# A decoder layer on one core: half of the attention moved among the expert gathers, and the first part of the mixer rewritten around a transposed x

## The reference, cut to what matters

```python
h = pad(concat([meta_tokens(16), x(1024)]))          # D_MODEL 1024
xn = rms_norm(h, norm1_g)
q, k, v, ga, gg = split(xn @ w_in)                    # 4 heads x (2 x 64), v: 4 x 128, conv: 2 x 512
p = softmax(q @ k.T / 8 - slope[head] * distance)     # causal, two components for each head
a = p[component 0] - lam * p[component 1]
attn = rms_norm(a @ v, attn_subln_g) * (1 - lam_init)
conv = silu(group_norm(depthwise_conv31(ga * sigmoid(gg))))
h = h + concat([attn, conv]) @ w_out
xn2 = rms_norm(h, norm2_g)
# experts, for every token and each of 8 heads:
s = (xn2 @ wq) @ subkeys.T                            # 2 x 128 scores
e = indices of the best 16 of the 16 x 16 best sums
w = softmax(best) * gelu(u_tab[e] . xn2)
h = h + sum(w * v_tab[e])
out = rms_norm(h, final_norm_g)[16:]
```

## Time and profile before

| what | value |
|---|---|
| time, three runs | 3162.5 us median, 3161.84 to 3164.97 |
| profiled execution, its own time | 3164.81 us |
| its span, first to last instruction | 3163.0 us |
| TensorE matmuls busy | 2352.9 us, 74% |
| VectorE busy | 2047.2 us, 65% |
| ScalarE busy | 1364.5 us, 43% |
| POOL busy | 1134.8 us, 36% |
| DMA | 1121.65 MB, mean 355 GB/s |
| mean granted TensorE clock | 0.833 of 2.4 GHz |

### The profile page before, as it was taken

The page is one execution under the profiler, slowest core; times in us unless marked ns, Lnnn a source line. Parts: engine busy times, 40 slices in busy tenths (PEclk is TensorE's granted clock), DMA queues, the critical chain, the costliest instruction groups (busy, mean ns, idle before and its releaser), DMA issues.

```text
span 3163.0 us, 36373 instructions
## 1 busy us (share of the span) xinstructions
PE 2352.9 (74%) x11880; PEld 897.3 (28%) x11880; DVE 2047.2 (65%) x4903; ACT 1364.5 (43%) x4011; POOL 1134.8 (36%) x1073
## 2 busy tenths in 40 slices
PE   8998987677677776777777767776777777777766
PEld 4655554322222222222222222222222222222211
DVE  1566673566666666666666666666666666666664
ACT  3143444344444444444444444444444444444443
POOL 1000000344444444443444434443444444444442
PEclk9999987788888878888888778877888888877776
DMA  3300000999999999999999999999999999999997
GB/s 110 120 27 27 20 7 25 390 426 427 427 426 423 426 426 413 427 425 426 419 418 424 426 424 421 424 427 425 410 425 426 426 414 423 426 424 426 420 426 332
DMA packets 184964, 1121.65 MB, mean 355 GB/s; under 512 B 19520, under 2 KB 45248, under 8 KB 53584
## 3 DMA queue, kind: packets, MB, share of 16 engines
q0 software_dynamic: 147456, 1073.81, 80.9%
q1 hardware_dynamic: 37328, 45.63, 4.3%
HBM read 1110.97 MB, written 8.39 MB: 354 GB/s over the span
## 4 chain that ended last, share of the span: by engine, by line
DMA 55%; PE 14%; ACT 5%; DVE 4%; issue 3%; POOL 2%; SPq 0%; DVEq 0%; ACTq 0%; POOLq 0%
DMA ring<-table,e_odd 28%; DMA ring<-table,e_even 26%; PE acc_odd L1350 5%; PE acc_even L1350 4%; DVE ring L1248 4%; PE qq_ps L1326 3%; PE proj L1307 2%; POOL ring L993 2%; ACT diag L1083 1%; ACT weight L1076 1%; ACT gelu L1100 1%; DMA wq_rest<-wq 1%; ACT L1100 1%; ACT L1058 0%; PE s_ps L1341 0%
## 5 line engine op out<-in xcount | busy, mean ns | idle before, releaser
L1248 DVE CUSTOM_DVE_ANT_0 ring<-ring,xn_odd 128x1024 f32<-128x1024 f32 x512 | 627.2, 1225 | 423.9 <-DMA ring<-table,e_odd 219.8
L1248 DVE CUSTOM_DVE_ANT_0 ring<-ring,xn_even 128x1024 f32<-128x1024 f32 x512 | 627.1, 1225 | 406.7 <-DMA ring<-table,e_odd 210.0
L1350 PE MATMUL acc_odd<-ring,diag 64*64 64x512 f32 x4096 | 674.5, 755 | 231.9 <-ACT diag L1083 231.1
L993 POOL DMA_INDIRECT ring<-table,e_even x512 | 549.6, 1074 | 767.8 <-PE acc_odd L1350 356.7
L1350 PE MATMUL acc_even<-ring,diag 64*64 64x512 f32 x4096 | 651.2, 732 | 216.1 <-ACT diag L1083 215.4
L993 POOL DMA_INDIRECT ring<-table,e_odd x512 | 552.5, 1079 | 712.7 <-PE acc_odd L1350 334.6
L1100 ACT ACTIVATE gelu<-dots 128x1 f32<-128x1 f32 x1024 | 207.5, 203 | 1349.5 <-DVE dots L1248 1345.9
L1083 ACT ACTIVATE diag<-pairs,weight 128x64 f32<-128x64 f32 x1024 | 356.0, 348 | 33.5
L1350 PEld LDWEIGHTS acc_odd<-ring,diag 64*64 64x64 f32 x4096 | 134.2, 156 | 635.2 <-ACT diag L1083 533.1
L1350 PEld LDWEIGHTS acc_even<-ring,diag 64*64 64x64 f32 x4096 | 132.6, 152 | 587.4 <-ACT diag L1083 473.7
L1326 PE MATMUL qq_ps<-wq_rest,xnT_cur 128*128 128x256 f32 x896 | 266.4, 436 | 8.4 <-DMA wq_rest<-wq 8.4
(11 more groups left out here) (191 smaller groups left out, 2112.1 us busy)
## 6 DMA issues: line engine op xcount, KB each, us to landing
w_slot<-w_in SPq DMA_DIRECT2D x16, 512.0 KB, 4.0
ring<-table,e_even POOLq DMA_INDIRECT x512, 15.5
ring<-table,e_odd POOLq DMA_INDIRECT x512, 15.1
wq_rest<-wq SPq DMA_DIRECT2D x1, 7168.0 KB, 23.4
w_out_s<-x SPq DMA_DIRECT2D x8, 512.0 KB, 3.9
w_out_s<-w_out SPq DMA_DIRECT2D x1, 4096.0 KB, 12.8
h_next<-x SPq DMA_DIRECT2D x8, 512.0 KB, 8.1
mix_t<-mix_dram SPq DMA_DIRECT2D x7, 512.0 KB, 7.8
```

The source lines that it names most:

```text
L993: pool.indirect_dma_start(out=ring[:, g % RING, :], out_offset=None, in_=table[:, :], in_offset=bass.IndirectOffsetOnAxis(ap=e_row[m % 2][ ...
L1248: dve.tensor_tensor_reduce(ring[:, g % RING, 0:D], ring[:, g % RING, 0:D], xn[(m // PH) % 2][:], 1.0, 0.0, ALU.mult, ALU.add, dots[:, k:k ...
L1350: ins = pe.matmul(acc[t % 2][ROWS[j], HALF[i]], diag[ROWS[i], g % DIAGS, :], ring[ROWS[i], g % RING, D + j * 512:D + (j + 1) * 512], start ...
```

## The change

In the mixer, x arrives transposed from the host (`xt`), and the weights in the layout in which they are used (`w_units`, `w_v`, `params`, `w_out`, `wq`). K[0] and K[1], the keys of heads 0 and 1, are computed from the raw x with weights that VectorE scales by norm1_g, K[0] while x lands, with the sums of squares as matmuls with a constant matrix beside it. VectorE multiplies both keys by the inverse norm on their way out of PSUM and then normalises `xT` in place. All loops are written out. Each convolution group's factors come from a variance matmul, a root over 1024 columns and a VectorE reciprocal over 1024 columns (`divide`). Attention in the mixer covers tiles 0 to 3 only (`EARLY`), 16 units; the last projection units are its fillers. Keys, late queries, values and bias are written to DRAM by POOL, as are the convolution and head outputs.

In the expert phase, tiles 4 to 7 of the four heads are 16 further units. Unit u fills a frame of 16 gathers that begins at step m = 8, k = 14, with offset o inside it: scores on TensorE at o 0, 2, 4, their reading on VectorE at o 1, 3, 5, exponentials at o 6, difference at o 9, transposes and outputs from o 10 to 15. `wide` (the room of `w_out_s`) holds their operands meanwhile, so the projections of tiles 1 to 3 are done in tile 0's steps, tiles 2 and 3 are put aside in DRAM, and `w_out` is loaded again afterwards. The scores use `acc_0`, so tiles 1, 2 and 3 share `acc_1` (`ACC_OF`), and finished accumulators are copied to `xn` before their norm (`last_copy`).

```diff
+EARLY = 4
+LATE = NT - EARLY
+ACC_OF = [0, 1, 1, 1, 0, 1, 0, 1]
+UNITS = HEADS * LATE
+FRAME0 = (1 * PH + 0) * TOPK + 14
# mixer, VectorE
-            def channel_factors(c):
-                dve.wait_ge(s_ystd, c + 1)
-                dve.reciprocal(y_rs[:], y_rs[:]).then_inc(s_yrec, 1)
+            def raw_keys(h, n):
+                lo, w = SEGS[n]
+                dve.wait_ge(p_seg, seg_at[K[h], n])
+                dve.tensor_tensor(kT_all[:, h, lo:lo + w], seg_bank(K[h], n)[:, 0:w], rstd[:, lo:lo + w],
+                                  ALU.mult).then_inc(p_evD, 1)
+            def normalise(k):
+                if k < KC - 1:
+                    dve.wait_ge(p_k1, k + 1)
+                else:
+                    dve.wait_ge(p_seg, seg_at[K[1], 2])
+                dve.scalar_tensor_tensor(out=xT[:, k, :], in0=xT[:, k, :], scalar=g1_cols[:, k:k + 1], in1=rstd[:],
+                                         op0=ALU.mult, op1=ALU.mult).then_inc(p_xn, 1)
+            def divide(c):
+                dve.wait_ge(p_root, 2 * (c + 1))
+                dve.reciprocal(y[c % 2][:], y[c % 2][:]).then_inc(p_yrec, 1)
+                dve.wait_ge(p_yrec, c + 1)
+                dve.tensor_tensor(yc[:], yc[:], y[c % 2][:], ALU.mult).then_inc(p_div, 1)
...
+            dve.wait_ge(p_std, 3)
+            dve.reciprocal(rstd[:], rstd[:]).then_inc(p_rstd, 1)
...
+            gated(0)
             taps(0, 0, TAPS)
+            gated(1)
+            taps(1, 0, 20)
+            centre(0, 0)
+            centre(0, 1)
+            taps(1, 20, TAPS)
+            divide(0)
+            gated(2)
...
+            for a in range(NU + 1):
+                h, i = divmod(a, EARLY)
+                if a >= 1:
+                    difference(a - 1)
...
# mixer, TensorE
+            for k in range(KC):
+                pe.wait_ge(p_x[k], 16)
+                raw_unit(0, k)
+                if k >= 1:
+                    mean_squares(k - 1)
+            mean_squares(KC - 1)
+            pe.wait_ge(p_ws, 2)
+            for k in range(KC):
+                raw_unit(1, k)
+            pe.wait_ge(p_const, 11)
+            for j in (G[0], A[0], G[1], A[1]):
                 for n in range(3):
+                    seg(j, n)
+            for m in range(5):
+                values(m)
+            for c in range(2):
+                group_means(c, 0)
+                group_means(c, 1)
+                for n in range(3):
+                    seg(G[c + 2], n)
+                group_variances(c, 0)
+                group_variances(c, 1)
+                for n in range(3):
+                    seg(A[c + 2], n)
...
+            for a in range(NU + 1):
+                h, i = divmod(a, EARLY)
+                if a < NU:
+                    scores(a)
+                if a >= 1:
+                    transposes(a - 1)
+                if a < len(FILLERS):
+                    seg(*FILLERS[a])
...
# expert phase, SyncE, tiles 1 to 4
+            sp.wait_ge(b_op, 4)
+            sp.dma_start(bias, dram["bias"]).then_inc(t_bias, 16)
+            keys_and_queries(0)
+            values(0)
+            put_aside(3)
+            fetch(2)
+            store(0)
+            keys_and_queries(1)
+            values(1)
+            keep_head(0)
...
+            sp.dma_start(w_out_s, w_out).then_inc(b_w2, 16)
+            store(2)
+            keep_head(3)
+            sp.wait_ge(t_hst, 16 * HEADS)
+            mix(4)
# expert phase, the order inside a step
+                    u, o = frame(m, k)        # divmod(16 m + k - FRAME0, 16)
                     combine(TOPK * m + k)     # TensorE
...
+                    if 0 <= u < UNITS:
+                        if o in (0, 2, 4) and o // 2 < len(chunks(TILES[u])):
+                            scores(u, o // 2)
+                        elif o == 10:
+                            transposes(u, 0)
+                        elif o == 12:
+                            output(u, 0)
+                            transposes(u, 1)
+                        elif o == 14:
+                            output(u, 1)
...
                     dot(g)                    # VectorE
...
+                        if o in (1, 3, 5) and o // 2 < len(chunks(TILES[u])):
+                            biased(u, o // 2)
+                        if o == 5:
+                            maxima(u)
+                        elif o == 9:
+                            difference(u)
...
+                        if o == 6:            # ScalarE, behind gate_exp
+                            exponentials(u)
+                        elif o in (11, 13):
+                            weights_out(u, (o - 11) // 2)
+                        elif o == 15:
+                            output_out(u)
+            def begin(t):
+                before = [s for s in range(t) if ACC_OF[s] == ACC_OF[t]]
+                if before:
+                    pe.wait_ge(b_acc, 2 * (before[-1] + 1))
```

More of the change, by code:

```diff
@@ L126, in mixer_phase @@
[L126 to L142, removed]
@@ new lines, in _ @@
+            gate(2, 2)
+            channel_roots(0, 0)
+            channel_roots(0, 1)
+            channel_output(0)
+            for n in range(3):
+                gate(3, n)
+            channel_squares(1)
+            channel_roots(1, 0)
+            channel_roots(1, 1)
+            channel_output(1)
+            for m in range(5, NT + 1):
+                values(m)
+            queries(0, 0)
+            channel_squares(2)
+            queries(0, 1)
+            queries(0, 2)
+            channel_roots(2, 0)
@@ new lines, in group_variances, with scores @@
+            def group_variances(c, b):
+                pe.wait_ge(p_csq, c + 1)
+                if c == 3 and b == 1:
+                    pe.wait_ge(p_root, 2 * c + 1)
+                pe.matmul(conv_bank(c, b)[:], group_mean[:], y[c % 2][:, b * 512:b * 512 + 512], start=True, stop=True
+                          ).then_inc(p_var, 1)
+            def scores(a):
+                h, i = divmod(a, EARLY)
+                if a == 0:
+                    pe.wait_ge(p_vs, NT + 1)
+                for n in range(2):
+                    if i == 0:
+                        wait_evicted(pe, K[h], n)
+                        wait_evicted(pe, Q[h], n)
+                for n, (lo, hi) in enumerate(chunks(i)):
@@ new lines, in output @@
+            def output(a):
+                h, i = divmod(a, EARLY)
+                cols = slice(h * P, (h + 1) * P)
+                pe.wait_ge(p_mts, a + 1)
+                pe.matmul(banks[7][:, P:2 * P], aT_meta[:], v_meta[:, cols], start=True, stop=False)
+                pe.wait_ge(p_ats, a + 1)
+                for b in range(i + 1):
+                    ins = pe.matmul(banks[7][:, P:2 * P], aT[:, b * P:(b + 1) * P], v_all[:, b, cols], start=False,
+                                    stop=(b == i))
+                ins.then_inc(p_pv, 1)
@@ new lines, in _ @@
+            sp.wait_ge(b_op, 3)
+            mix(3)
+            put_aside(2)
+            tokens(3)
+            sp.wait_ge(b_op, 4)
[7 more added lines that the diff above has]
+            values(1)
+            keep_head(0)
+            sp.wait_ge(b_hin, 3)
+            fetch(3)
+            keys_and_queries(2)
+            values(2)
@@ new lines, in output @@
+            def output(u, part):
+                first, count = 4 * part, min(4, TILES[u] + 1 - 4 * part)
+                if part == 0:
+                    pe.wait_ge(t_mts, u + 1)
+                    pe.wait_ge(t_v, 32 * (u // LATE + 1))
+                    pe.matmul(proj[1][:, P:2 * P], aT_meta, v_meta, start=True, stop=False)
+                pe.wait_ge(t_ats, 2 * u + part + 1)
+                for b in range(count):
+                    ins = pe.matmul(proj[1][:, P:2 * P], aT[:, b * P:(b + 1) * P], v_head[:, first + b, :], start=False,
+                                    stop=(first + b == TILES[u]))
+                if part == 1:
+                    ins.then_inc(t_pv, 1)
```

1681 lines of the change are left out of this document (962 added, 719 removed).

## The result

The changed kernel took 3116.36 us (3115.82 to 3117.82, 4 runs) against 3162.89 for the kernel before beside it: a ratio of 0.9853 [0.9842, 0.9865]. It is 46.5 us faster, where 95.5 were forecast, and 8 us above the range of 3038 to 3108. The span is 3114.8 instead of the predicted 3068, so 46.8 us are to be found. Three places of the trace show where they may lie.

The account below looks back on a forecast made before the run. TensorE's order was taken to bound the mixer and the DMA engines the gathers. 3163.0 - 137 (mixer) + 33 (added bytes) + 8 (stalls) + 1 (end) = 3068, read as 3067 us; range 3038 to 3108.

Parts of the forecast that it names:

- The mixer's end at 414: Mixer: TensorE's work in order sums to 386 us, plus 28 idle, ending at 414 instead of 551; gain 137.
- The passage from mixer to first gather: Between last projection and first gather: 25.6 us kept, since the same loads go out; counted as nothing, bounds -3 and +2.
- 2.38 us a megabyte: Gathers: DMA engines are the bound, and each megabyte costs 2.38 us, as in the profile of the kernel before.
- Added bytes 33: Beside the gathers: 13.1 MB of added loads and stores cost 33 us, between 31 and 39 by two prices.
- stalls 8: Attention frames beside the gathers: VectorE's waits at 36 score chunks, mostly absorbed by the ring, cost 8 us, bounds 0 and 32.
- end 1: End of the kernel: the copy ahead of the last squares costs 1 us.
- (a): Rival, mixer: TensorE and VectorE wait for each other more and wide reciprocals uncover; mixer ends at 440, time 3093; 14%.
- (b): Rival, gathers: the ring runs down partly, 3 us a frame, 48 instead of 8, time 3107; 10%.
- (c): Rival, gathers: the added bytes hide, as in pauses of the gathers, time 3034; 8%.
- (d): Rival, gathers: the ring does not cover the score chunks, 169 us instead of 8, slower than before at 3229; 3%.
- (e): Rival, gathers: TensorE at its lower clock becomes the bound in frames, 51 against 40.3 us, time 3240; 3%.
- (f): Rival, whole kernel: the change does nothing, the mixer's tail replaces what is saved, same time; 2%.

Follow-up runs that it names:

- gf_first: The changed kernel with the two loads of gf_half moved ahead of the seven loads of wq; 3096.53 us, ratio 0.979.
- ring_at_256: The changed kernel with 192 bytes of padding ahead of the ring and 64 behind, so it starts at a multiple of 256; 3081.27 us, ratio 0.9743.
- before_ring_off: The kernel before with 64 bytes of padding ahead of its ring and 192 behind, nothing else; 3197.33 us, ratio 1.0116.
- both_mended: The changed kernel with the edits of gf_first and ring_at_256 together; 3065.82 us, ratio 0.9696.
- scores_first: both_mended with the scores of a late unit ahead of the combine of the same gather in TensorE's order; 3060.05 us, ratio 0.9676.

## Why the prediction was wrong, point by point

Taken in the spans: 414 + 25.6 + 2586.2 (first gather to end before) + 42 = 3067.8 was forecast, 3114.8 measured.

- **The mixer's end at 414, first gather near 440.** The mixer's end held, at 414.7, in part by luck: with the 10 us of waiting taken out of its 386, the working had 376 busy and 38 idle, against 382.0 and 33.0, and the two misses nearly cancel. Its detail was half wrong: "They are covered by segments and values of TensorE" fails for the divisions of groups 2 and 3, behind which TensorE waits 8.0 and 5.6 us; the sum came out because the 7 us for the first units and the last head and the 21 of the handovers held enough. Its bounds of 398 and 437 don't follow from the bounds of its terms, which give 386 - 3 + 21 = 404 and 386 + 2 + 21 + 25 = 434. The reciprocal of 1040, taken as 6 by the slope of the narrow ones, measured 6.65.
The Trainium skill, page VectorE: DVE Perf Modes, section Walkthrough: the 8-slice pipeline in each mode, gave the estimate of 8.6 that the prediction weighed; the measurement, 6.65, lies below it and decides.
- **"The passage from mixer to first gather is kept ... I count nothing" is the first step that failed.** It cost 20 us (gf_first). I had the order of SyncE's loads in the two kernels, and the trace of the kernel before had its DMA engines at work through the passage. I took from that that order made no difference; but the order decided which load landed last. The bounds of -3 and +2 were for the bytes, which had not changed, and not for who waits for them. `b_par` counts three loads, g_row and the two of gf_half, and VectorE waits for all of them at once; the change had put wq between them.
- **The gathers at the price of before, "2.38 us a megabyte", is the second, and the larger: 35 us.** No term of the working was for the place of a buffer. It was taken as given that 1073.7 MB which the change doesn't touch would take the time that they had taken. They took 1.4% longer, since allocations ahead of the ring had moved it by 64 bytes (ring_at_256, before_ring_off). No view of the profile before could price this; the addresses, which the diff changes, could have raised the question.
- **Added bytes 33, stalls 8, end 1.** In both_mended the stretch from first gather to end is 3061.0 - 440.5 = 2620.5, 34.3 more than before, against 42. This rests on two single executions; by the medians it is some 5 us more, 39. The 13.15 MB cost 23 to 29 of it at 1.75 to 2.17 us a megabyte, and the waits at chunks some 6. Both terms were a little high. The wait for mix(4), put at 2 or 3 us and into no term, is 5.7 us of TensorE in both_mended; what of it reaches the end, no run separates.
- **The misses together:** 3116.4 - 3067 = 49.4 us were missing. The two edits of both_mended give back 50.5 (singly 19.8 and 35.1, so some 4 us of them overlap), and what is left of the working was 1 too high.
- **The rivals.** (a) held in kind, for two divisions, not in size: the mixer ended at 414.7 and not at 440. (b), a ring that runs down, fell: both_mended and scores_first show some 6 and not 48. (c) held to a quarter with the waits in place, to a tenth at most without. (d) fell: 36 chunks behind combines cost some 6 us and not 169. (e) fell: with attention in the frames the granted clock is 0.89, higher than the 0.83 of the earlier trace rows, and the DMA share 1.01. (f) fell: the interval of the ratio ends at 0.9865. None of the rivals named what happened, and the range, built from them, was too narrow on its upper side.

## What to carry to other kernels

When a kernel's time is one long stream of transfers, write down where its buffers start, before and after a change: here small allocations ahead of them cost 35 us, about as much as all the bytes and waits that the change adds beside the gathers. Where a change touches the order of loads, follow the smallest one that something waits for, and put it ahead of the large ones; equal bytes in a passage say nothing about who waits. Where VectorE serves TensorE in small turns, cut a long instruction such as a wide reciprocal into pieces and put them in different turns.

## What the runs showed of the hardware

- 64 bytes in the start of the gathers' destination (138560 instead of 138496 or 138752) change the rate of saturated DMA engines from 424 to 418 and from 426 to 421 GB/s, at a share of 1.01 in every case: the share says that the engines are full, and not that they work at their best rate. The GB/s column has to be read beside it.
- A reciprocal of 1024 takes 6546 ns, 6.4 ns an element, where the step from 8 to 16 elements in the earlier trace rows gives 5.3; the taps of the same width took 1285 ns here and 1322 in the earlier trace rows, for which no run gives a reason.
- Loads beside saturated gathers can cost less than the gathers' own 2.38 us a megabyte: 7.1 MB were worth 12.4 us, 1.75 a megabyte, with the waits of both_mended in place. Without them it was 15.4, which is within the noise of the full price.
- A wait of TensorE can cost more than its length: without the two long ones it was busy 377.2 us instead of 382.0 for the same instructions, at a mean granted clock of 1.00 instead of 0.98.
